# Two compression products of one transformer block: interleaved on two column halves of TensorE, or one after the other into one half

## The chip, the cores and the metric

One core of a Trainium2 chip runs the whole block. The metric is the device time of one execution in microseconds (us); lower is better. The engines are PE (TensorE), DVE (VectorE), ACT (ScalarE), POOL (GpSimd) and SP (SyncE, which issues most DMAs here). SBUF and PSUM have 128 partitions.

## The reference, cut to what matters

The block is a feed-forward layer, a token mixer and a second feed-forward layer over 512 tokens of width 1024, all in float32. In the mixer, keys and values of two KV groups are compressed: blocks of 32 tokens, 16 apart, become one key or value each (31 blocks per group), through a small two-layer network.

```
def compress(k, pos, w1, w2):
    b_, g_, s_, d_ = k.shape
    kc = k.reshape(b_, g_, s_ // CMP_STRIDE, CMP_STRIDE, d_)
    blocks = jnp.concatenate([kc[:, :, :-1], kc[:, :, 1:]], axis=3) + pos
    blocks = blocks.reshape(b_, g_, -1, CMP_BLOCK * d_)
    return jax.nn.gelu(blocks @ w1) @ w2
...
    kc = compress(k_cmp, cmp_pos_k, cmp_k_w1, cmp_k_w2)
    vc = compress(v_cmp, cmp_pos_v, cmp_v_w1, cmp_v_w2)
```

`blocks @ w1` has a contraction of 2048 (32 tokens times 64) and 256 hidden columns. The results feed a softmax attention over the 31 compressed blocks, one of three attention branches.

## The kernel before, in words

Activations lie feature by token: `h` is eight tiles of 128 features x 512 tokens. Weights stream in panels of 128 x 1024 float32 from HBM. ACT copies each panel into `w_hi` in a reduced format (fp32r) and POOL makes the remainder `w_lo` (L430); a product of full precision is three fp32r matmuls, `w_hi*h_hi`, `w_hi*h_lo`, `w_lo*h_hi` (L506 to L508). A panel over `h` is 24 such matmuls of 512 columns. Panels have four slots; SP loads, ACT and POOL split up to three panels ahead of PE.

The order of work is written out by hand per engine, with semaphores between them. In the mixer PE runs the panels `kc`, `vc`, `u0` to `u3`, then the compression's first layer (L696), the panel `gate`, the transposes of the hidden layer (L703), the panel `q0`, the second layer (L710, L714), the transposes of the gates (L721), `q1` to `q3`, the scores against the compressed keys (L731), more panels, and then the attention proper, in which PE, DVE, ACT and POOL hand tiles to each other (L761 scores, L812 transposes, L839 weighted sums).

The first layer works as follows. DVE writes `blocks` (L1487), in which partition is (parity of the token, feature) and the free dimension is (k or v and half of the block, pair of tokens, group and block). For each of the 16 pairs of tokens PE takes 64 columns of `blocks` as the stationary operand (31 blocks of each group and two columns that mean nothing) and streams `w1k` or `w1v`, 256 columns. The key product goes to partitions 0 to 63 of PSUM bank 2, the value product to partitions 64 to 127 of the same columns, and the code alternates key and value for every pair. These are float32 matmuls, not fp32r; each shows in the trace as two instructions.

The hidden layer is thus 128 x 256: rows are k then v. The tanh form of GELU follows on it: Square on ACT (L1099), two DVE operations (L1522, L1523), a Tanh on ACT with its table load (L1101), one DVE operation (L1526). PE waits for that (`cmp_act`) only after the panel `gate`. Two transposes of 128 x 128 (L703) put it into bank 3, and DVE copies it to `hidden` (L1528), which PE waits for after the panel `q0`.

Of the kernel before, what the change touches and what calls it, by code (L numbers as in the profile page):

```python
# [31 lines left out]
ALU = mybir.AluOpType  # L32
# [3 lines left out]
P = 128  # L36
# [8 lines left out]
HPG = HEADS // GROUPS  # L45
STRIDE = 16
N_CMP = T // STRIDE - 1
CPAD = 32
HID_T = 2
PAIRS = 16  # L50
# [74 lines left out]
def build(nc, xT, cols, ada_w, ada1, ffn_in, ffn_out, mix_w, pool_w, branch_w, mixout_w,  # L125
          w1, w2, pos, ident_in, dist_in, cbias_in, cmask_in, icnt_in, out):
    with ExitStack() as ctx:
        def at(name, shape, offset, dt=F32):
            return nc.alloc_sbuf_tensor_at(name, shape, dt, offset=offset)
# [11 lines left out]
        scr = at("scr", [P, 4, T], O_SCR)  # L141
# [7 lines left out]
        R = O_REGION  # L149
# [7 lines left out]
        V = at("V", [P, 2, TT, P], R + 12288)  # L157
        vT = at("vT", [P, 2, T], R + 16384)
        w1v = at("w1v", [P, PAIRS, 256], R)
        blocks = at("blocks", [P, 4 * 512 + 1], R + 20480)  # L160
        PT = at("PT", [P, 2, 2, PT_LEN], O_ADARAW)
        Pr = at("Pr", [P, 2, 2, P_LEN], R + 20480)
        pads = at("pads", [P, 4, 528], R + 30720)
        hidden = at("hidden", [P, 4, 64], R + 39168)
        cbias = at("cbias", [P, TT, HEADS, N_CMP], R + 40960)
        PcT = at("PcT", [P, GROUPS, T], R + 40960)
        dist = at("dist", [P, T], R + 45056)
        abias = [at("abias0", [P, 2, T], R + 47104), at("abias1", [P, 2, T], R + 16384)]
        Pc = at("Pc", [P, TT, HEADS, CPAD], R + 51200)
        cmask = at("cmask", [P, TT, CPAD], R + 55296)  # L170
        G = at("G", [P, TT, 24], R + 55808)
# [8 lines left out]
        w1k = at("w1k", [P, PAIRS, 256], R + 73728)  # L180
# [5 lines left out]
        ident = at("ident", [P, P], o)  # L186
# [7 lines left out]
        w2s = at("w2s", [P, 2, HID_T, HEAD], o + 2816)  # L194
        icnt = at("icnt", [P, 4, 16], o + 3840)
        kcB = at("kcB", [P, 2 * N_CMP], o + 4096)
        st = at("st", [P, 8, TT], o + 4352)
# [3 lines left out]
        psum = ctx.enter_context(nc.psum_tensor("psum", [P, 8, T], F32))  # L201

        def bank(n, w=T):
            return psum[:, n, 0:w]

        def sem(name):
            return ctx.enter_context(nc.semaphore(name))
# [70 lines left out]
        cmp_act = sem("cmp_act")  # L278
# [223 lines left out]
        def _(pe):  # L502
            def product(o_, wslot, kk, xh, xl, first, last):

                ws = slice(kk * P, (kk + 1) * P)
                pe.matmul(o_, w_hi[:, wslot, ws], xh, start=first, stop=False)  # L506
                pe.matmul(o_, w_hi[:, wslot, ws], xl, start=False, stop=False)  # L507
                return pe.matmul(o_, w_lo[:, wslot, ws], xh, start=False, stop=last)  # L508
# [180 lines left out]

            pe.wait_ge(mixc_landed, 16 * 5)  # L690
            pe.wait_ge(kv_blocks, 8)
            for i in range(PAIRS):
                half = i // 8
                for kv in range(2):
                    first = 512 * (2 * kv + half) + 64 * (i % 8) + half
                    ins = pe.matmul(psum[64 * kv:64 * kv + 64, 2, 0:256], blocks[:, first:first + 64],  # L696
                                    (w1k, w1v)[kv][:, i, :], start=(i == 0), stop=(i == PAIRS - 1))
            ins.then_inc(cmp_hidden, 1)
            k8_panel("gate")

            pe.wait_ge(cmp_act, 1)
            for kt in range(HID_T):
                ins = pe.transpose(psum[:, 3, P * kt:P * kt + P], scr[:, 0, P * kt:P * kt + P], ident[:, :])  # L703
            ins.then_inc(cmp_turned, 1)
            k8_panel("q0")

# [1 line left out]
            for g in range(GROUPS):  # L708
                for kt in range(HID_T):
                    pe.matmul(psum[64 * g:64 * g + 64, 2, 0:N_CMP], w2s[:, 0, kt, :],  # L710
                              hidden[:, 2 * kt, 32 * g:32 * g + N_CMP], start=(kt == 0), stop=(kt == 1))
            for g in range(GROUPS):
                for kt in range(HID_T):
                    ins = pe.matmul(psum[0:31, 2, 64 + 64 * g:128 + 64 * g],  # L714
                                    hidden[:, 2 * kt + 1, 32 * g:32 * g + N_CMP], w2s[:, 1, kt, :],
                                    start=(kt == 0), stop=(kt == 1))
            ins.then_inc(cmp_kv, 1)

# [1 line left out]
            for t in range(TT):  # L720
                ins = pe.transpose(psum[:, 4, P * t:P * t + P], vT[:, 0, t * P:(t + 1) * P], ident[:, :])  # L721
# [6 lines left out]
            for t in range(TT):  # L728
                for j in range(HPG):
                    col = ((t % 2) * HPG + j) * 2 * N_CMP  # L730
                    ins = pe.matmul(psum[:, 6 + t // 2, col:col + 2 * N_CMP], qT[:, j, t * P:(t + 1) * P],  # L731
                                    kcB[:, :], start=True, stop=True)
# [37 lines left out]
            for v in range(2):  # L770
                pe.wait_ge(act_evac, MIX8.index("vslc") - 1 + v)
                for t in range(TT):
                    ins = pe.transpose(psum[:, 2 + v, P * t:P * t + P], vT[:, v, t * P:(t + 1) * P], ident[:, :])
                ins.then_inc(v_turned, 1)

            p = pidx["poolw"]
            pe.wait_ge(split_done, p + 1)
            pe.wait_ge(pool_split, 4)
            for g in range(4):
                ins = product(bank(4 + g), p % 4, g, pool_hi[:, g, :], pool_lo[:, g, :], True, True)  # L780
# [5 lines left out]
            for g in range(GROUPS):  # L786
                pe.wait_ge(poolout_split, g + 1)
                for t in range(TT):
                    ins = pe.transpose(psum[:, 4 + g, P * t:P * t + P],
                                       Pc[:, t, HPG * g:HPG * g + HPG, :].rearrange("p h n -> p (h n)"),  # L790
                                       ident[:, :])
# [68 lines left out]
            for m in range(KT):  # L860
                p = B_BRANCH + 3 * m
# [17 lines left out]
                for k in range(4):  # L879
                    ins = product(bank(b + 3), p % 4, 4 + k, o_hi[:, k, :], o_lo[:, k, :], k == 0, k == 3)  # L880
# [3 lines left out]
            for m in range(KT):  # L884
                p = B_MIXOUT + m
# [5 lines left out]
                for k in range(KT):  # L891
                    if m == 0:
                        pe.wait_ge(br_split, k + 1)
                    ins = product(bank(m % 2), p % 4, k, mixed_hi[:, k, :], mixed_lo[:, k, :],
                                  k == 0, k == KT - 1)
# [7 lines left out]
        def _(act):  # L903
# [190 lines left out]
            act.wait_ge(pool_delta, 5)  # L1094
            act.activation(pool_hi[:, 3, :], pads[:, 3, 16:528], ACT.Copy).then_inc(pool_hi_done, 1)
            act.wait_ge(cmp_hidden, 1)
            hb = psum[:, 2, 0:256]
            sq = scr[:, 1, 0:256]
            act.activation(sq, hb, ACT.Square).then_inc(cmp_sq, 1)  # L1099
            act.wait_ge(cmp_arg, 1)  # L1100
            act.activation(sq, sq, ACT.Tanh, scale=GELU_A).then_inc(cmp_tanh, 1)  # L1101
# [85 lines left out]
        def _(dve):  # L1187
# [279 lines left out]
            def taken(name):  # L1467
                return B_MIX + MIX.index(name) + 1

            dve.wait_ge(h_split, 16)  # L1470
            for i in range(4):
                ins = dve.memset(pads[:, i, 0:16], 0.0)
            ins.then_inc(pool_delta, 1)
            dve.memset(Pc[:, :, :, N_CMP:CPAD], 0.0)
            dve.memset(blocks[:, 4 * 512:], 0.0)
            for kv, name in enumerate(("kc", "vc")):

                dve.wait_ge(panels_used, taken(name))
                for half in range(2):
                    for r in range(2):  # L1480
                        for g in range(GROUPS):
                            src = psum[64 * g:64 * g + 64, kv, r:T:2].rearrange("p (n i) -> p i n", i=8)
                            dst = blocks[64 * r:64 * r + 64, 0:4 * 512].rearrange("p (n i c) -> p n i c", n=4, c=64)\
                                [:, 2 * kv + half, :, 32 * g:32 * g + 32]
                            pp = posv[64 * r:64 * r + 64, kv:kv + 1, 8 * half:8 * half + 8]\
                                .rearrange("p o i -> p i o").broadcast_to([64, 8, 32])
                            ins = dve.tensor_tensor(dst, src, pp, ALU.add)  # L1487
                            if r == 1:
                                ins.then_inc(kv_blocks, 1)
            for g, w in enumerate(WINDOWS):  # L1490
# [25 lines left out]
            dve.tensor_tensor(pool_lo[:, 3, :], pads[:, 3, 16:528],  # L1516
                              pool_hi[:, 3, :].bitcast(F32), ALU.subtract).then_inc(pool_split, 1)

            hb = psum[:, 2, 0:256]
            sq = scr[:, 1, 0:256]  # L1520
            dve.wait_ge(cmp_sq, 1)
            link(dve.tensor_scalar(sq, sq, GELU_B, 1.0, ALU.mult, ALU.add))  # L1522
            dve.tensor_tensor(sq, sq, hb, ALU.mult).then_inc(cmp_arg, 1)  # L1523
            dve.memset(kcB[:, :], 0.0)
            dve.wait_ge(cmp_tanh, 1)
            dve.scalar_tensor_tensor(scr[:, 0, 0:256], sq, 1.0, hb, ALU.add, ALU.mult).then_inc(cmp_act, 1)  # L1526
            dve.wait_ge(cmp_turned, 1)
            dve.tensor_copy(hidden[:, :, :].rearrange("p n c -> p (n c)"), psum[:, 3, 0:256])\  # L1528
               .then_inc(cmp_hidden_T, 1)
            dve.wait_ge(cmp_kv, 1)  # L1530
            for g in range(GROUPS):
                rows = slice(64 * g, 64 * g + 64)
                ins = dve.tensor_scalar(kcB[rows, N_CMP * g:N_CMP * g + N_CMP], psum[rows, 2, 0:N_CMP], 0.5, None, ALU.mult)
            ins.then_inc(cmp_kv_taken, 1)
            for r in range(4):
                ins = dve.tensor_scalar(VC[32 * r:32 * r + 31, :], psum[0:31, 2, 64:192], 0.5, None, ALU.mult)
# [20 lines left out]
            for t in range(TT):  # L1557
                ins = dve.tensor_tensor(Pc[:, t, :, 0:N_CMP], Pc[:, t, :, 0:N_CMP], over_blocks(cst[:, 0, :], t), ALU.subtract)
# [7 lines left out]
            for t in range(TT):  # L1566
                ins = dve.tensor_tensor(Pc[:, t, :, 0:N_CMP], Pc[:, t, :, 0:N_CMP], over_blocks(cst[:, 2, :], t), ALU.mult)
            link(ins)
            for t in range(TT):
                ins = dve.tensor_tensor(Pc[:, t, :, 0:N_CMP], Pc[:, t, :, 0:N_CMP],  # L1570
                                        cmask[:, t:t + 1, 0:N_CMP].broadcast_to([P, 8, N_CMP]), ALU.mult)
# [118 lines left out]
def _constants():  # L1690
# [10 lines left out]
    cb = cb.reshape(TT, P, HEADS, N_CMP).transpose(1, 0, 2, 3)  # L1701
    cm = np.zeros((T, CPAD), np.float32)
    cm[:, :N_CMP] = d >= 0
    cm = cm.reshape(TT, P, CPAD).transpose(1, 0, 2)
    ic = np.stack([1.0 / np.minimum(np.arange(16) + 1, w) for w in WINDOWS]).astype(np.float32)
# [73 lines left out]
```

## Time and profile before

| | us |
|---|---|
| three runs | 1179.96, 1178.36, 1177.53 (median 1178.36) |
| profiled execution, its own time | 1179.96 |
| its span, first to last instruction | 1178.1 |
| PE busy | 1117.6 (95%) |
| POOL busy | 539.3 (46%) |
| DVE busy | 512.9 (44%) |
| ACT busy | 400.1 (34%) |
| mean granted TensorE clock | 0.973 |

The span ends 1.9 us short of the execution's own time. Busy time of PE counts from the first to the last moment at which any of its pipelined matmuls is open, so it says that PE had work, not that the array was full. PEld is the load of the stationary operand. An instruction's duration includes its way through the pipeline; how fast instructions follow each other is read from their start times. Shapes in PE rows read as stationary operand (partitions*columns), then the streamed operand (partitions x columns).

### The profile page before, as it was taken

To read this page: it belongs to the slowest core of one execution; us is meant where nothing else is said; L and a number is where in the kernel's file an instruction comes from. 1 tells how busy PE (TensorE), PEld (TensorE's weight loads), DVE (VectorE), ACT (ScalarE), POOL (GpSimd) and SP (SyncE) were. 2 spreads that over 40 slices of the span, in tenths; PEclk is the share of its full clock that TensorE was granted. 3 is DMA by queue.
4 is the path that set the end of the run, shared out by engine and by line. 5 is a ranking of instruction groups with operands and counts; after the bars stand their busy time and mean duration, and the time that the engine had idled before them with its cause. 6 is when DMAs were issued, how large, how long until landed. Compare 5 with 4: busy or idle time off the path is not lost.

```text
span 1178.1 us, 14475 instructions
## 1 busy us (share of the span) xinstructions
PE 1117.6 (95%) x5182; PEld 886.6 (75%) x5182; DVE 512.9 (44%) x830; ACT 400.1 (34%) x608; POOL 539.3 (46%) x268
## 2 busy tenths in 40 slices
PE   6999999999999889999999999969999999999992
PEld 3788888888888657875478888848888888888881
DVE  3567656321221366267837776661622222111116
ACT  3453323232222163247722333344423222222212
POOL 1334544444444363367725543544544544444423
PEclk8899999999999989999999999989999999999996
DMA  9446555323333522210036554313333333333311
GB/s 373 143 138 201 186 183 174 112 92 95 86 97 96 194 106 86 63 45 28 19 114 218 188 178 143 125 36 125 125 125 125 107 110 103 87 97 98 98 32 72
DMA packets 46991, 142.06 MB, mean 121 GB/s; under 512 B 5472, under 2 KB 5984, under 8 KB 45664
## 3 DMA queue, kind: packets, MB, share of 16 engines
q1 hardware_dynamic: 45504, 136.07, 34.9%
q10 hardware_dynamic: 1440, 5.35, 1.2%
q8 instruction: 30, 0.49, 0.2%
q14 instruction: 17, 0.14, 0.0%
HBM read 139.31 MB, written 2.10 MB: 120 GB/s over the span
## 4 chain that ended last, share of the span: by engine, by line
PE 76%; issue 10%; POOL 6%; DVE 5%; ACT 2%; DMA 1%; SPq 0%; POOLq 0%; ACTq 0%; DVEq 0%
PE psum L506 24%; PE psum L507 23%; PE psum L508 23%; POOL w_lo L430 3%; POOL Pr L465 1%; DMA ada_first<-in_ada 1%; POOL h_lo L488 1%; PE psum L590 1%; PE psum L537 1%; ACT Pr L1119 1%; PE psum L812 1%; PE psum L696 1%; DVE X L1290 1%; PE psum L523 0%; PE psum L761 0%
## 5 line engine op out<-in xcount | busy, mean ns | idle before, releaser
L430 POOL TENSOR_TENSOR w_lo<-raw,w_hi 128x1024 fp32r<-128x1024 f32 x184 | 452.4, 2462 | 551.9 <-ACT w_hi L916 551.5
L506 PE MATMUL psum<-h_hi,w_hi 128*128 128x512 f32 x952 | 375.8, 395 | 9.0 <-POOL h_lo L488 8.8
L507 PE MATMUL psum<-h_lo,w_hi 128*128 128x512 f32 x952 | 373.1, 392 | 0.0
L508 PE MATMUL psum<-h_hi,w_lo 128*128 128x512 f32 x952 | 372.9, 392 | 0.0
L916 ACT ACTIVATE w_hi<-raw 128x1024 fp32r<-128x1024 f32 x184 | 192.7, 1051 | 160.1 <-PE psum L508 104.0
L506 PEld LDWEIGHTS psum<-h_hi,w_hi 128*128 128x128 f32 x952 | 180.2, 189 | 55.3 <-POOL h_lo L488 9.2
L508 PEld LDWEIGHTS psum<-h_hi,w_lo 128*128 128x128 f32 x952 | 180.3, 189 | 38.0
L507 PEld LDWEIGHTS psum<-h_lo,w_hi 128*128 128x128 f32 x952 | 180.5, 190 | 36.4
L1318 DVE SCALAR_TENSOR_TENSOR acc<-ada_raw,cact,acc 128x512 f32<-128x512 f32 x98 | 138.3, 1447 | 19.0 <-DMA ada_raw<-in_ada_w 18.6
L506 PE MATMUL psum<-act_hi,w_hi 128*128 128x512 f32 x352 | 137.3, 390 | 0.0
L508 PE MATMUL psum<-act_hi,w_lo 128*128 128x512 f32 x352 | 137.0, 389 | 0.0
L507 PE MATMUL psum<-act_lo,w_hi 128*128 128x512 f32 x352 | 137.0, 389 | 0.0
L1386 DVE SCALAR_TENSOR_TENSOR X<-psum,mod,X 128x512 f32<-128x512 f32 x24 | 18.0, 750 | 217.3 <-PE psum L508 217.2
L1018 ACT ACTIVATE act_hi<-scr 128x512 f32 (+1 forms) x42 | 26.6, 632 | 187.3 <-DVE scr L1348 187.3
L1339 DVE SCALAR_TENSOR_TENSOR scr<-scr,psum 128x512 f32<-128x512 f32 x44 | 30.2, 686 | 123.6 <-ACT scr L1025 123.6
L508 PEld LDWEIGHTS psum<-act_hi,w_lo 128*128 128x128 f32 x352 | 66.1, 188 | 13.7
L507 PEld LDWEIGHTS psum<-act_lo,w_hi 128*128 128x128 f32 x352 | 66.1, 188 | 13.7
L506 PEld LDWEIGHTS psum<-act_hi,w_hi 128*128 128x128 f32 x352 | 66.1, 188 | 13.5
L1348 DVE TENSOR_TENSOR scr<-scr,psum 128x512 f32<-128x512 f32 x44 | 30.2, 686 | 89.0 <-PE psum L508 88.8
L1025 ACT ACTIVATE scr<-psum 128x512 f32<-128x512 f32 x44 | 26.1, 593 | 97.6 <-PE psum L508 97.6
L465 POOL TENSOR_SCALAR Pr<-Pr,pscl 128x128 f32<-128x128 f32 (+2 forms) x48 | 44.8, 950 | 19.2 <-DVE pscl L1594 19.2
L936 ACT ACTIVATE scr<-X 128x512 f32<-128x512 f32 x24 | 15.2, 634 | 104.8 <-DVE X L1386 104.8
(206 smaller groups left out, 986.0 us busy)
## 6 DMA issues: line engine op xcount, KB each, us to landing
raw<-in_ffn_in SPq DMA_DIRECT2D x88, 512.0 KB, 3.3
ada_raw<-in_ada_w SPq DMA_DIRECT2D x112, 256.0 KB, 3.6
raw<-in_mix_w SPq DMA_DIRECT2D x31, 512.0 KB, 3.3
raw<-in_ffn_out SPq DMA_DIRECT2D x32, 448.0 KB, 3.3
ada_first<-in_ada SPq DMA_DIRECT2D x8, 1024.0 KB, 16.2
raw<-in_ffn_out SPq DMA_DIRECT2D x16, 512.0 KB, 3.5
raw<-in_branch_w SPq DMA_DIRECT2D x8, 512.0 KB, 4.0
raw<-in_mixout_w SPq DMA_DIRECT2D x8, 512.0 KB, 3.3
```

The costliest lines, as they stand in the source:

```text
L430: gp.tensor_tensor(w_lo[:, slot, :], raw[:, slot % 2, :], w_hi[:, slot, :].bitcast(F32), ALU.subtract).then_inc(split_done, 1)
L465: gp.tensor_scalar(pr, pr, pscl[:, n:n + 1], None, ALU.mult).then_inc(probs_pool, 1)
L506: pe.matmul(o_, w_hi[:, wslot, ws], xh, start=first, stop=False)
L507: pe.matmul(o_, w_hi[:, wslot, ws], xl, start=False, stop=False)
L508: return pe.matmul(o_, w_lo[:, wslot, ws], xh, start=False, stop=last)
L916: act.activation(w_hi[:, slot, :], raw[:, slot % 2, :], ACT.Copy).then_inc(split_hi, 1)
L1018: act.activation(act_hi[:, c - 1, :] if isinstance(c, int) else act_hi[:, bass.ds(c - 1, 1), :].rearrange("p o t -> p (o t)"), scr[:, 1 - ...
L1025: act.activation(scr[:, c2, :], bank(2 * c2 if b is None else b), ACT.Tanh, scale=0.5).then_inc(tanh_done, 1)
L1318: dve.scalar_tensor_tensor(a, ada_raw[:, q % 3, :], sc, a, ALU.mult, ALU.add).then_inc(ada_used, 1)
L1339: dve.scalar_tensor_tensor(scr[:, c2, :], scr[:, c2, :], 1.0, bank(b0), ALU.add, ALU.mult).then_inc(gated, 1)
L1348: dve.tensor_tensor(scr[:, c2, :], scr[:, c2, :], bank(b0 + 1), ALU.mult).then_inc(hidden_made, 1)
L1386: dve.scalar_tensor_tensor(X[:, m, :], bank(y_bank + m % 2), mod[:, 4, m:m + 1], X[:, m, :], ALU.mult, ALU.add).then_inc(z_done, 1)
```

## The change

The two products are no longer interleaved. All 16 key matmuls run first, into partitions 0 to 62 and columns 0 to 255 of bank 2; then all 16 value matmuls into the same partitions and columns 256 to 511. The stationary operand has 63 columns (`CROWS`), not 64, so the memset of one spare element of `blocks` goes. The hidden layer is 63 x 512 and no longer 128 x 256, and the five GELU operations run on that shape. Its transposes are four of 63 x 128 rather than two of 128 x 128, and `hidden` is indexed as k0, k1, v0, v1. One line is added at the top of the file, so most later lines are one or two numbers further down.

```diff
+CROWS = 32 + N_CMP
...
-        blocks = at("blocks", [P, 4 * 512 + 1], R + 20480)
+        blocks = at("blocks", [P, 4, PAIRS // 2, 64], R + 20480)
...
-            for i in range(PAIRS):
-                half = i // 8
-                for kv in range(2):
-                    first = 512 * (2 * kv + half) + 64 * (i % 8) + half
-                    ins = pe.matmul(psum[64 * kv:64 * kv + 64, 2, 0:256], blocks[:, first:first + 64],
-                                    (w1k, w1v)[kv][:, i, :], start=(i == 0), stop=(i == PAIRS - 1))
+            for kv in range(2):
+                for i in range(PAIRS):
+                    half = i // 8
+                    ins = pe.matmul(psum[0:CROWS, 2, 256 * kv:256 * kv + 256],
+                                    blocks[:, 2 * kv + half, i % 8, half:half + CROWS], (w1k, w1v)[kv][:, i, :],
+                                    start=(i == 0), stop=(i == PAIRS - 1))
...
-            for kt in range(HID_T):
-                ins = pe.transpose(psum[:, 3, P * kt:P * kt + P], scr[:, 0, P * kt:P * kt + P], ident[:, :])
+            for n in range(4):
+                ins = pe.transpose(psum[:, 3, 64 * n:64 * n + CROWS], scr[0:CROWS, 0, P * n:P * n + P],
+                                   ident[0:CROWS, 0:CROWS])
...
-                              hidden[:, 2 * kt, 32 * g:32 * g + N_CMP], start=(kt == 0), stop=(kt == 1))
+                              hidden[:, kt, 32 * g:32 * g + N_CMP], start=(kt == 0), stop=(kt == 1))
...
-                                    hidden[:, 2 * kt + 1, 32 * g:32 * g + N_CMP], w2s[:, 1, kt, :],
+                                    hidden[:, 2 + kt, 32 * g:32 * g + N_CMP], w2s[:, 1, kt, :],
...
-            hb = psum[:, 2, 0:256]
-            sq = scr[:, 1, 0:256]
+            hb = psum[0:CROWS, 2, :]
+            sq = scr[0:CROWS, 1, :]
...
-            dve.memset(blocks[:, 4 * 512:], 0.0)
...
-            dve.scalar_tensor_tensor(scr[:, 0, 0:256], sq, 1.0, hb, ALU.add, ALU.mult).then_inc(cmp_act, 1)
+            dve.scalar_tensor_tensor(scr[0:CROWS, 0, :], sq, 1.0, hb, ALU.add, ALU.mult).then_inc(cmp_act, 1)
             dve.wait_ge(cmp_turned, 1)
-            dve.tensor_copy(hidden[:, :, :].rearrange("p n c -> p (n c)"), psum[:, 3, 0:256])\
+            dve.tensor_copy(hidden[:, :, 0:CROWS], psum[:, 3, 0:256].rearrange("p (n c) -> p n c", c=64)[:, :, 0:CROWS])\
```

On PE, at the first layer of the compression, the program had this before: the last matmul of panel `u3`, then the products with `w1k` and `w1v` in turn (32 in all; the first four and the last two stand here), then the panel `gate`.

```order
L508 MATMUL psum<-h_hi_50,w_lo_54 128x512
L696 MATMUL psum<-w1k_100,blocks_79 64x256
L696 MATMUL psum<-w1v_78,blocks_79 64x256
L696 MATMUL psum<-w1k_100,blocks_79 64x256
L696 MATMUL psum<-w1v_78,blocks_79 64x256
...
L696 MATMUL psum<-w1k_100,blocks_79 64x256
L696 MATMUL psum<-w1v_78,blocks_79 64x256
L506 MATMUL psum<-h_hi_50,w_hi_53 128x512
```

The same place of PE's program after the change, from the end of `u3` to the first product of `gate`:

```order
L508 MATMUL psum<-h_lo_51,w_hi_53 128x512
L509 MATMUL psum<-h_hi_50,w_lo_54 128x512
L696 MATMUL psum<-w1k_100,blocks_79 63x256 x16
L696 MATMUL psum<-w1v_78,blocks_79 63x256 x16
L507 MATMUL psum<-h_hi_50,w_hi_53 128x512
```

Sixteen pairs became two runs of sixteen; the count of matmuls and what lies around them is the same.

One panel later on PE, where the hidden layer (`scr`) is turned against the identity (`ident`), the program had before, between `gate` and `q0`:

```order
L506 MATMUL psum<-h_hi_50,w_hi_53 128x512
L507 MATMUL psum<-h_lo_51,w_hi_53 128x512
L508 MATMUL psum<-h_hi_50,w_lo_54 128x512
L703 MATMUL psum<-ident_104,scr_57 128x128 x2
L506 MATMUL psum<-h_hi_50,w_hi_53 128x512
```

and it has after the change:

```order
L507 MATMUL psum<-h_hi_50,w_hi_53 128x512
L508 MATMUL psum<-h_lo_51,w_hi_53 128x512
L509 MATMUL psum<-h_hi_50,w_lo_54 128x512
L704 MATMUL psum<-ident_104,scr_57 128x63 x4
L507 MATMUL psum<-h_hi_50,w_hi_53 128x512
```

Two transposes became four of 63 streamed columns each, at the same place.

## Rows read from the trace of the kernel before

**Rows 1.** The page: busy time by engine (us, share), and the last chain by engine.
```profile
PE 1117.6 (95%) x5182; PEld 886.6 (75%) x5182; DVE 512.9 (44%) x830; ACT 400.1 (34%) x608; POOL 539.3 (46%) x268
PE 76%; issue 10%; POOL 6%; DVE 5%; ACT 2%; DMA 1%; SPq 0%; POOLq 0%; ACTq 0%; DVEq 0%
```

**Rows 2.** PE in order of time: start us, duration us, line, tiles, shapes, count.
```profile
454.24 0.39 PE L508 MATMUL psum<-h_hi,w_lo 128*128 128x512 f32 x1
454.56 0.43 PE L696 MATMUL psum<-w1k,blocks 128*64 128x256 f32 x1
454.57 0.43 PE L696 MATMUL psum<-w1v,blocks 128*64 128x256 f32 x1
454.83 0.38 PE L696 MATMUL psum<-w1k,blocks 128*64 128x256 f32 x1
...
461.31 0.38 PE L696 MATMUL psum<-w1v,blocks 128*64 128x256 f32 x1
461.62 0.50 PE L506 MATMUL psum<-h_hi,w_hi 128*128 128x512 f32 x1
```

**Rows 3.** Groups of PE by shape: count, busy us, mean ns of one.
```profile
L696 PE MATMUL psum<-w1k,blocks 128*64 128x256 f32 x32 | 7.1, 381 | 0.0
L696 PE MATMUL psum<-w1v,blocks 128*64 128x256 f32 x32 | 7.1, 381 | 0.0
...
L839 PE MATMUL psum<-PT,V 128*64 128x384 f32 x32 | 6.5, 486 | 0.0
...
L839 PE MATMUL psum<-PT,V 128*64 128x128 f32 x32 | 3.1, 273 | 0.0
```

**Rows 4.** PE in order of time, around the two transposes.
```profile
466.28 0.39 PE L508 MATMUL psum<-h_hi,w_lo 128*128 128x512 f32 x1
...
466.96 0.39 PE L508 MATMUL psum<-h_hi,w_lo 128*128 128x512 f32 x1
467.20 0.38 PE L703 MATMUL psum<-ident,scr 128*128 128x128 f32 x2
...
467.64 0.39 PE L507 MATMUL psum<-h_lo,w_hi 128*128 128x512 f32 x1
```

**Rows 5.** PE in order of time, compressed scores with 62 streamed columns.
```profile
491.69 3.75 PE L731 MATMUL psum<-kcB,qT 128*128 128x62 f32 x32 [0.78 <-ACT qT L1108]
495.25 0.47 PE L506 MATMUL psum<-h_hi,w_hi 128*128 128x512 f32 x1
```

**Rows 6.** ACT in order of time, around the GELU.
```profile
454.67 0.60 ACT L1089 ACTIVATE pads<-psum 128x512 f32<-128x512 f32 x1 [3.37 <-PE psum L508]
...
461.74 0.38 ACT L1099 ACTIVATE scr<-psum 128x256 f32<-128x256 f32 x1 [1.04 <-PE psum L696]
462.14 1.28 ACT L1101 ACT_TABLE_LOAD   x1
463.43 0.42 ACT L1101 ACTIVATE scr<-scr 128x256 f32<-128x256 f32 x1
```

**Rows 7.** DVE in order of time, around the GELU.
```profile
459.13 0.69 DVE L1508 SCALAR_TENSOR_TENSOR pads<-scr,pads 128x512 f32<-128x512 f32 x1
...
462.48 0.42 DVE L1523 TENSOR_TENSOR scr<-scr,psum 128x256 f32<-128x256 f32 x1
...
463.88 0.42 DVE L1526 SCALAR_TENSOR_TENSOR scr<-scr,psum 128x256 f32<-128x256 f32 x1 [0.91 <-ACT scr L1101]
```

**Rows 8.** Stretch after the first layer: length, busy of PE, PEld, DVE, ACT, POOL; clock; DMA.
```profile
461.70:600.00 138.30, 130.31 (x740) 89.17 (x741) 79.21 (x243) 71.44 (x184) 82.67 (x67) 1.00 0.13 43
```

**Rows 9.** Longest wait of PEld in that stretch that another engine ends: total us, times, longest.
```profile
PEld psum L812 <- POOL Pr L465: 10.7, 19, 1.0
```

**Rows 10.** Stretches of PE alone: length, PE busy, granted clock, DMA share, GB/s.
```profile
457.00:460.00 3.00, 3.00 (x30) 1.00 0.03 11
...
410.00:415.00 5.00, 3.08 (x4) 0.50 0.99 426
...
420.00:425.00 5.00, 4.64 (x14) 0.78 0.00 0
```

More of the change, by code:

```diff
@@ L1482, in _ @@
                             src = psum[64 * g:64 * g + 64, kv, r:T:2].rearrange("p (n i) -> p i n", i=8)
-                            dst = blocks[64 * r:64 * r + 64, 0:4 * 512].rearrange("p (n i c) -> p n i c", n=4, c=64)\
-                                [:, 2 * kv + half, :, 32 * g:32 * g + 32]
+                            dst = blocks[64 * r:64 * r + 64, 2 * kv + half, :, 32 * g:32 * g + 32]
                             pp = posv[64 * r:64 * r + 64, kv:kv + 1, 8 * half:8 * half + 8]\
@@ L1517, in _ @@
                               pool_hi[:, 3, :].bitcast(F32), ALU.subtract).then_inc(pool_split, 1)
-            hb = psum[:, 2, 0:256]
-            sq = scr[:, 1, 0:256]
+            hb = psum[0:CROWS, 2, :]
+            sq = scr[0:CROWS, 1, :]
             dve.wait_ge(cmp_sq, 1)
```

## The prediction

> **What bounds the kernel now.** I read the page first. PE is busy for 95% of the span and carries 76% of the chain that ended last, the next engine 6% [rows 1]. So time added to PE's own program counts in full unless PE stood idle behind it for someone who would now be ready. Then PE in order of time around L696 [rows 2]. The panel `u3` ends with a matmul started at 454.24, the first key product and the first value product start at 454.56 and 454.57, the second key product at 454.83, the last value product at 461.31, and the panel `gate` at 461.62. PE does not wait inside this stretch. The reader is to see that a key and a value instruction start together.
>
> **Is this really two at once?** It decides everything, so it needs a second view. There are 32 instructions on `w1k` and 32 on `w1v` [rows 3], twice the 16 + 16 matmuls of the program. From the second key instruction (454.83) to the last value one (461.31) lie 30 steps of pairs: 6.48 / 30 = 0.216 us a step (starts are rounded, and the last pair starts with the last value row). Either one instruction takes 0.108 and the two go one after the other, or each takes 0.216 and they run side by side. The groups by shape decide. On the same kind of tile, L839 takes 273 ns with 128 streamed columns and 486 ns with 384; the 256 further columns cost 213 ns, and L696 with 256 columns stands at 381, on the same line [rows 3]. So streaming 256 float32 columns occupies a tile for 0.213 us, and 64 instructions fit into 7.06 us (461.62 - 454.56) only because two column halves stream at once. A slope of duration cannot be a delay that instructions share, so I trust it.
>
> By the Trainium skill's page "TensorEngine Tiling (Array Packing)", section "Key Properties", different tiles load and multiply in parallel; the trace agrees with its 0.01 us between the paired starts.
>
> **The change part by part.**
>
> 1. Products in one half. All 32 matmuls (64 instructions) now write from partition 0, so they share the same columns of the array and queue behind each other. Before, 32 steps of 0.215 (6.86 to 6.9 us); after, 64 steps. Added: 32 x 0.2145 = 6.9 us. Bounds of the step: 0.213, the pure streaming time, gives 6.8 with nothing lost; the upper end takes the spacing of the full panels, whose three matmuls from 466.28 to 466.96 take 0.227 each [rows 4]. They stream at a rate of their own, so only the excess over 0.213, 0.014 us, is carried over: 64 x 0.014 = 0.9 more, 7.8 in all. I take 6.9, since each column half already held 0.215 in the row that is the very operation. One column less in the stationary operand changes nothing, because it streams against the same 256 columns. The gaps at either end (454.24 to 454.56, 461.31 to 461.62) stay.
>
> 2. Transposes, four for two. From the last L508 of `gate` (466.96) to the second matmul of `q0` (467.64) are 0.68 us, where two ordinary steps take 0.45; so two transposes cost 0.23 [rows 4]. For instructions with few streamed columns and 128 stationary ones, L731 has a spacing of (495.25 - 491.69) / 32 = 0.111 us [rows 5]. Two more transposes at 0.111 add 0.22. They have 63 rows now, and PE's tiling may change around them; the trace's nearest row is the step from `u3` to L696, 0.32 instead of 0.227, which is 0.09 for a change of tiles [rows 2]. Two of those would bring 0.4. Lower end 0 (four times half the streamed columns), upper 0.5; I take 0.25.
>
> 3. GELU on 63 x 512. Time goes by elements per partition, which double. On ACT, 256 columns take 0.38 and 512 take 0.60 [rows 6]; on DVE 0.42 against 0.69 [rows 7]. The chain from the end of L696: Square 0.60, then the table load 1.28 side by side with two DVE operations, which at 0.6 + 0.69 now just fill it, Tanh about 0.62, the last DVE operation 0.69, and some 0.1 between them: 3.3 us, where it took 461.74 to 464.30, 2.6 us [rows 6, 7]. PE asks for it after `gate`, at 467.2, 5.5 us after the products [rows 4]. So 2.2 us of cover are left, and the cost is 0. Without that panel the 0.7 us would show. ACT's next weight copy stands behind the Tanh and moves some 0.4 us later; it is for a panel three ahead of PE. Cost 0.
>
> 4. The copy to `hidden`, 252 elements for 256, covered by the panel `q0`; the memset of one element that goes, DVE long before. 0.
>
> 5. What is given back. From 461.7 to 600 PE is busy 130.3 of 138.3 us [rows 8], so 8 us of idleness could in principle take up the 6.9. But I read its largest case, PE's transposes L812 waiting for POOL's scaling L465, 19 times and at most 1.0 us each [rows 9]; that scaling waits for scores that PE itself makes two steps earlier. All of it moves with PE. Weight panels are split three ahead of PE and PE did not wait for one here. Given back: 0, at most 0.5.
>
> Sum: 6.9 + 0.25 = 7.15 us. The profiled execution would go from 1179.96 to 1187.1, its span from 1178.1 to 1185.25. That execution was the highest of three, 1.6 above the median; the forecast is for a median, 1178.36 + 7.15 = 1185.5.
>
> **Rivals.**
>
> A. The pairs were never side by side: one instruction occupies PE for 0.108 us, and order alone changes. Then L696 stays at 7 us and only the transposes add 0.25, with 1178.6 as the time. Against it stands the slope of 213 ns per 256 columns [rows 3]. 3%.
>
> B. Serial loads. In one column half a stationary operand may have to wait for the matmul in flight. L731 is bound by such loads: 0.111 us for 128 columns, so 0.056 for 63 [rows 5]. Then a step is 0.214 + 0.056 = 0.27, 64 steps 17.3 us, and the change 17.3 - 6.9 + 0.25 = +10.7, at 1189.0. Against it: the panels' 128-column loads would make their step 0.213 + 0.111 = 0.32, and it is 0.227 [rows 4]; and L696 shows 0.215 within each half. 5%. The Trainium skill, "TensorE: Matmul & The Clock Gate", section "The mechanism", states this rule: loads overlap a matmul in flight only where the row group differs, and here all rows are the same ones. The panels of this trace speak against it.
>
> C. The clock. With one half of the columns at work the granted clock may fall to its lower level, 1.2 GHz. From 410 to 415 us the granted clock was 0.50, which is that level, while PE was busy 3.08 of 5 us; in L696, without a gap, it was 1.00 [rows 10]. What lowers it here goes with pauses, and the change brings none; no row shows half the columns at work for 14 us. If it fell in the middle, the second half of the products takes 6.9 us more; when PE resumed after its pause around 410 us, the stretch from 420 to 425 had 0.78 [rows 10], so over 1 us is lost at the return, say 2. Total +7.15 + 9 = 16 us, at 1194.5. 5%.
>
> D. Given back, so not slower. PE's 8 idle microseconds after 461.7 [rows 8] would be waits for work that does not depend on PE's position, with POOL behind on splitting weights and late with its scaling. Then PE arriving 6.9 later finds all ready. To end below the time before, it would have to return over 7.15 of the 8.0, and it decides from the point at which POOL is idle before L465; POOL is busy 82.7 of 138.3 us there [rows 8], so it is not behind. It would give 1178.36 + 7.15 - 8.0 = 1177.5. 1%. A part of this, some 3 us given back (1182.5), 3%.
>
> **How the numbers follow.** The forecast (rigid shift, 6.8 to 8.3 us) has 83%, A 3, B 5, C 5, D 4. Terms at their ends: 6.8 + 0 - 0.5 = 6.3 and 7.8 + 0.5 = 8.3, which is 1184.7 to 1186.7. Three runs before spread by 2.4 us, so a median is uncertain by about 1 on both sides of the comparison: 1183.6 to 1188.1. A range from 1183.5 to 1188.3 leaves out most of B, all of A, C and D. No change that a measurement can tell is within 0.2%, 2.4 us. Slower by more: forecast, B, C and the mild part of D, 95%; within: A and noise, 4%; faster 1%.
>
> **What the profile after would show.** L696 as two blocks of 32 instructions each, with no two starts together, spacing 0.213 to 0.227, and 13.7 to 14.6 us from its first start to the first of `gate`. Spacing 0.27 is B, a granted clock under 1.00 there is C, 7 us in all is A. Step 2: from the last matmul of `gate` to the second of `q0` 0.9 us rather than 0.68. Step 3: the last GELU operation ends about 3.3 us after L696, and PE has no wait before the transposes; a wait there would make it wrong. Step 5: from the transposes to the end of the span all distances as before, and PE idle again about 8 us in the same stretch. The forecast is wrong if the span grows by less than 6 or more than 9 us.

## The result

The changed kernel takes 1185.21 us (median of four runs, 1184.42 to 1186.39), the kernel before, run beside it, 1177.94 us (median of four, 1177.31 to 1179.96): +7.27 us, a ratio of 1.0058 with a 95% interval of 1.0044 to 1.0073, which is 5.2 to 8.6 us. The forecast was +7.15, at 1185.5. The profiled execution took 1185.08 us, with a span of 1183.2.

### The profile page after: what moved, and what is told of

Same layout as the page of the kernel before. It is cut to its first block, busy times and chain, and to the rows that moved or that the text cites. A ratio compares the mean times of both kernels' runs of the same rounds, so it can differ in the third digit from the quotient of the medians.

```text
span 1183.2 us, 14478 instructions
## 1 busy us (share of the span) xinstructions
PE 1121.2 (95%) x5184; PEld 887.8 (75%) x5184; DVE 513.9 (43%) x829; ACT 400.5 (34%) x608; POOL 539.6 (46%) x268
## 4 chain that ended last, share of the span: by engine, by line
PE 87%; DVE 5%; ACT 2%; POOL 2%; issue 2%; DMA 2%; SPq 0%; ACTq 0%; DVEq 0%; POOLq 0%
PE psum L507 27%; PE psum L508 27%; PE psum L509 27%; DMA raw<-in_ffn_in 2%; PE psum L696 1%; POOL Pr L466 1%; POOL h_lo L489 1%; PE psum L591 1%; ACT Pr L1121 1%; PE psum L814 1%; PE psum L841 1%; PE psum L538 1%; DVE X L1292 1%; PE psum L524 1%; PE psum L763 0%
## 5 line engine op out<-in xcount | busy, mean ns | idle before, releaser
L508 PEld LDWEIGHTS psum<-act_lo,w_hi 128*128 128x128 f32 x352 | 66.1, 188 | 13.6
L1332 DVE TENSOR_TENSOR act_lo<-scr,act_hi 128x512 f32 (+1 forms) x44 | 37.1, 843 | 36.2 <-ACT act_hi L1020 34.8
```

Source lines behind the costliest of these rows:

```text
L1332: dve.tensor_tensor(lo_, scr[:, b, :], hi.bitcast(F32), ALU.subtract).then_inc(act_split, 1)
```

## The profile after, beside the rows of before

PE in order of time, at the first layer of the compression (start us, duration us, line, tiles, shapes, count; equal neighbours are merged into one row):

```profile
452.93 7.12 PE L696 MATMUL psum<-w1k,blocks 128*63 128x256 f32 x32
459.89 7.07 PE L696 MATMUL psum<-w1v,blocks 128*63 128x256 f32 x32
466.89 0.50 PE L507 MATMUL psum<-h_hi,w_hi 128*128 128x512 f32 x1
```

It answers to [rows 2]. The two kinds no longer start together: 32 key instructions, then 32 value instructions. From the first of them to the first matmul of `gate` are 13.96 us, where it was 7.06. One step is 13.96 / 64 = 0.218 us with the gap at the end counted in, and (459.89 - 452.93) / 32 = 0.2175 without it; each column half had 0.216 before.

PE, ACT and DVE after that, up to the transposes:

```profile
472.23 0.39 PE L509 MATMUL psum<-h_hi,w_lo 128*128 128x512 f32 x1
472.55 0.46 PE L704 MATMUL psum<-ident,scr 63*128 63x63 f32 x4
472.94 0.50 PE L507 MATMUL psum<-h_hi,w_hi 128*128 128x512 f32 x1
473.27 0.39 PE L508 MATMUL psum<-h_lo,w_hi 128*128 128x512 f32 x1
```

```profile
467.00 0.59 ACT L1101 ACTIVATE scr<-psum 63x512 f32<-63x512 f32 x1 [7.93 <-PE psum L696]
467.60 1.28 ACT L1103 ACT_TABLE_LOAD   x1
468.90 0.63 ACT L1103 ACTIVATE scr<-scr 63x512 f32<-63x512 f32 x1
```

```profile
467.62 0.42 DVE L1522 TENSOR_SCALAR scr<-scr 63x512 f32<-63x512 f32 x1 [7.83 <-ACT scr L1101]
468.07 0.68 DVE L1523 TENSOR_TENSOR scr<-scr,psum 63x512 f32<-63x512 f32 x1
469.56 0.68 DVE L1526 SCALAR_TENSOR_TENSOR scr<-scr,psum 63x512 f32<-63x512 f32 x1 [0.74 <-ACT scr L1103]
```

From the last matmul of `gate` to the second of `q0` are now 1.04 us (472.23 to 473.27); in [rows 4] they were 0.68. The GELU runs from 467.00 to 470.24, 3.24 us; in [rows 6, 7] it took 2.56. It ends 2.3 us before PE asks for it, so PE waits for nothing.

The stretch of 138.3 us that follows `gate`'s start, in the form of [rows 8]:

```profile
466.90:605.20 138.30, 130.33 (x741) 89.03 (x741) 79.83 (x243) 71.70 (x183) 82.67 (x67) 1.00 0.14 43
```

PE is busy 130.33 us of it, before 130.31, and its wait for POOL's scaling, the one of [rows 9], is 10.2 us in 18 pieces. Nothing was given back in this stretch.

For comparisons finer than a run's spread I use one distance within a trace: from the first product of the first layer to the first score against the compressed keys. Before, 454.56 [rows 2] to 491.69 [rows 5] is 37.13 us; after, 452.93 to 497.32 is 44.39. The difference is 7.26 us. That the medians differ by 7.27 is agreement within their interval of 5.2 to 8.6; the match of the last digit is luck. The spans differ by only 5.1 us, for two other reasons. The profiled execution after reached the first layer 1.63 us earlier, in a part where the two programs are alike and where the granted clock fell and came back at other moments (18 to 21 us: 1.00 where it was 0.50 before the change; 29 to 59 us: 0.91 against 0.88). And from the scores to the end it took 0.5 us less: one wait of PE for a weight panel split by POOL, 0.3 us, is missing, as it also is in e11 below, and the rest arises around 790 us, where the clock falls while PE pauses. All distances below are from the first product to the first score.

## The experiments

The theory was the forecast's: two products run together because of their place, that is, because they lie in different column halves of the array. Rivals were order (alternation as such), serial loads of the stationary operand, and the clock.

**Both in one half, but alternating (e3).** The changed kernel with the loops exchanged and the value product in bank 3 (the GELU then reads both banks; those lines are left out here):

```diff
-            for kv in range(2):
-                for i in range(PAIRS):
+            for i in range(PAIRS):
+                for kv in range(2):
...
-                    ins = pe.matmul(psum[0:CROWS, 2, 256 * kv:256 * kv + 256],
+                    ins = pe.matmul(psum[0:CROWS, 2 + kv, 0:256],
```

> The changed kernel, with key and value products alternating as before the change, but both in the same column half; the value product goes to PSUM bank 3 instead of the upper half of bank 2. Theory (place): as slow as the changed kernel, first layer 13.9 us, 7.2 us slower than before. Rival (order): what the change lost is the alternation, for instance because two products on one accumulator in a row wait for each other; then the first layer is near 7.1 us here and the kernel near the time of before.

Measured: ratio to before 1.0077 (1.0060 to 1.0094), distance 44.39, as in the changed kernel, first layer 13.96 us. PE in order of time:

```profile
451.06 0.65 PE L696 MATMUL psum<-w1k,blocks 128*63 128x256 f32 x2
451.54 0.59 PE L696 MATMUL psum<-w1v,blocks 128*63 128x256 f32 x2
451.97 0.59 PE L696 MATMUL psum<-w1k,blocks 128*63 128x256 f32 x2
452.40 0.59 PE L696 MATMUL psum<-w1v,blocks 128*63 128x256 f32 x2
```

The reader sees that a float32 product is two instructions, and that each pair of one kind starts 0.43 us (the first time 0.48) after the pair of the other kind, never with it. Alternation alone brings nothing; place is needed.

**Both halves kept, order changed (e1, e2, e10, e11).** The kernel before, with turns of 16, 4, 8 and 2 products:

```diff
-            for i in range(PAIRS):
-                half = i // 8
+            for c in range(0, PAIRS, 16):
                 for kv in range(2):
...
+                    for i in range(c, c + 16):
+                        half = i // 8
```

This is e1; e2, e10 and e11 have 4, 8 and 2 in place of 16.

> The kernel before, both column halves of the array kept, but all 16 key products first and then all 16 value products. Theory (place): what makes two products run together is that they lie in different column halves. How far apart they may stand in PE's program is open. If PE starts instructions strictly in order, no value product starts before the last key product has started; the first layer then takes 63 steps of 0.215 = 13.6 us instead of 7.06, and the kernel is 6.6 us slower than before. If PE can reach over 32 queued instructions, the first layer stays at 7.1 us and the kernel at the time of before. Rival (order is nothing, place is all) predicts 7.1 us.

> The kernel before, both column halves kept, in turns of 4 key products and 4 value products. Strictly in order with one instruction open per half: each turn of 8 instructions per half overlaps with the other half only at its edges, where the last key and first value instruction start together; 64 starts less 7 shared ones = 57 steps of 0.215, 12.2 us, the kernel about 5.2 us slower than before. If PE reaches over 8 instructions but not over 32, it is 7.1 us here and 13.6 us with turns of 16.

> The kernel before, both column halves kept, in turns of 8 key and 8 value products. Theory drawn from the turns of 16 and 4: PE starts an instruction of the other half over 3 queued ones of its own, so at each of the 3 borders between turns 4 instructions of each half run side by side; 64 - 3 x 4 = 52 steps, 11.2 us of first layer and 4.1 us more than before. Rival (a reach that ends between 8 and 32 instructions): all turns up to some length near 7.1 us.

> The kernel before, both column halves kept, in turns of 2 key and 2 value products, which is 4 instructions each. Theory (reach over 3 queued instructions): every step has a partner but for the first and last few; 32 steps and 1 to 4 more, first layer 7.1 to 7.9 us, kernel within 0.9 us of before. Rival (strictly in order): 64 - 15 = 49 steps, 10.5 us.

| products per turn | first layer us | distance us | to before | ratio (95%) |
|---|---|---|---|---|
| 1 (before) | 7.06 | 37.13 | | |
| 2 (e11) | 7.11 | 37.19 | +0.06 | 0.9992 (0.9979 to 1.0004) |
| 4 (e2) | 8.31 | 38.41 | +1.28 | 1.0010 (1.0000 to 1.0020) |
| 8 (e10) | 11.54 | 41.62 | +4.49 | 1.0033 (1.0012 to 1.0053) |
| 16 (e1) | 13.15 | 43.23 | +6.10 | 1.0067 (1.0050 to 1.0083) |

So place is needed but does not suffice: with both halves in use, turns of 16 lose nearly all that the change loses. By the device times e1 is even further from before (ratio 1.0067, about 7.9 us); its profiled execution shows why that can be: behind the scores, outside the distance, the granted clock fell to 0.50 for some 6 us (498 to 505) and 2.8 us were lost, which no other profiled execution of this table shows. PE around the border between the two turns of e1:

```profile
452.94 6.47 PE L697 MATMUL psum<-w1k,blocks 128*64 128x256 f32 x29
459.04 0.43 PE L697 MATMUL psum<-w1v,blocks 128*64 128x256 f32 x1
459.25 0.38 PE L697 MATMUL psum<-w1k,blocks 128*64 128x256 f32 x1
459.31 0.38 PE L697 MATMUL psum<-w1v,blocks 128*64 128x256 f32 x1
459.46 0.38 PE L697 MATMUL psum<-w1k,blocks 128*64 128x256 f32 x1
459.52 0.38 PE L697 MATMUL psum<-w1v,blocks 128*64 128x256 f32 x1
459.68 0.38 PE L697 MATMUL psum<-w1k,blocks 128*64 128x256 f32 x1
459.74 6.42 PE L697 MATMUL psum<-w1v,blocks 128*64 128x256 f32 x29
```

and at the start of e2:

```profile
453.92 1.29 PE L697 MATMUL psum<-w1k,blocks 128*64 128x256 f32 x5
454.84 0.43 PE L697 MATMUL psum<-w1v,blocks 128*64 128x256 f32 x1
455.05 0.38 PE L697 MATMUL psum<-w1k,blocks 128*64 128x256 f32 x1
```

In e1 the first value instruction starts with key instruction 29 of 32 and ahead of three that precede it in the program; in e2 with number 5 of 8, again ahead of three. For e1 a strict order had given 13.6 us, the measured first layer is 13.15. For e2 both values of the expectation were wrong, 12.2 us by a strict order and 7.1 if PE reaches over 8; the measured 8.31 lies between. The rule "ahead of at most three queued instructions of the other half" was drawn from these two and then forecast turns of 8: 52 steps, 11.2 us. e10 gave 11.54, and its first value instruction starts with key instruction 13 of 16:

```profile
454.97 3.02 PE L697 MATMUL psum<-w1k,blocks 128*64 128x256 f32 x13
457.62 0.43 PE L697 MATMUL psum<-w1v,blocks 128*64 128x256 f32 x1
```

e11 lay inside its 7.1 to 7.9. The count of steps leaves out two things. Before the change 32 steps of 0.215 are 6.9 us and the first layer takes 7.06, so about 0.2 belongs to its two ends. And every border between turns costs about 0.06 us more: in e1 the value stream follows 0.06 us behind the key stream. With both, e10 comes to 11.2 + 0.2 + 3 x 0.06, e2 (36 steps, 7 borders) to 8.3 and e1 (60 steps, one border) to 13.1, all within 0.1 us of what was measured.

**One kind of product nearly left out (e4, e5).** Of the 16 value products only the first is done, in the kernel before (e4, first pair of lines) and in the changed one (e5, second pair); the compressed values are then not the reference's.

```diff
-                for kv in range(2):
+                for kv in range(2 if i == 0 else 1):
...
-                for i in range(PAIRS):
+                for i in range(PAIRS if kv == 0 else 1):
```

> The kernel before without 15 of the 16 value products (the compressed values are then not the reference's). Theory: they ran beside the key products, so leaving them out saves nothing: first layer 6.9 to 7.1 us, kernel within 0.3 us of before. Rival (the pair was one after the other at 0.108 each): the first layer falls to 3.6 us and the kernel is 3.3 us faster.

> The changed kernel without 15 of its 16 value products (the compressed values are then not the reference's). Theory: each was a step of its own, 30 instructions of 0.215, so it is 6.5 us faster than the changed kernel and 0.8 us slower than before (the two steps left of the value, and four transposes for two). Rival (they are hidden in part): less than 6 us is saved.

In the kernel before, the distance is 37.12, 0.01 less than with all products (ratio 1.0003, 0.9993 to 1.0013): 15 products left out, nothing saved. In the changed kernel it falls from 44.39 to 37.91, by 6.48 us for 30 instructions, 0.216 each. That is 0.8 us more than the distance before, as expected; the device times (ratio 0.9998, 0.9986 to 1.0010) can't tell it from before. PE in e4 and in e5:

```profile
452.01 0.43 PE L696 MATMUL psum<-w1k,blocks 128*64 128x256 f32 x1
452.01 0.43 PE L696 MATMUL psum<-w1v,blocks 128*64 128x256 f32 x1
...
452.49 6.64 PE L696 MATMUL psum<-w1k,blocks 128*64 128x256 f32 x30
459.06 0.50 PE L506 MATMUL psum<-h_hi,w_hi 128*128 128x512 f32 x1
```

```profile
461.07 0.59 PE L696 MATMUL psum<-w1v,blocks 128*63 128x256 f32 x2
461.60 0.50 PE L507 MATMUL psum<-h_hi,w_hi 128*128 128x512 f32 x1
```

Rival A, that the pairs were never side by side, is ruled out by e4: at 0.108 us each the 30 instructions left out would have saved 3.2 us.

**Products doubled (e6).** The changed kernel with each run of 16 done twice, `for kv in (0, 0, 1, 1):`.

> The changed kernel with each run of 16 products done twice (the second overwrites the first). Theory: 64 more instructions of 0.213 to 0.217, 13.7 us more than the changed kernel, about 20.9 us more than before, with the granted clock at 1.00 throughout the 27.6 us. Rival (clock): with half the columns at work for so long the granted clock falls to the lower level somewhere in the stretch; the added time is then over 16 us, up to 27, and steps of 0.43 us appear.

Ratio 1.0171 (1.0154 to 1.0188), distance 58.20: 13.81 us more than the changed kernel for 64 instructions, 0.216 each. The granted clock in the stretch (length, PE busy, clock, DMA share, GB/s):

```profile
455.00:460.00 5.00, 5.00 (x25) 1.00 0.09 33
...
475.00:480.00 5.00, 5.00 (x25) 1.00 0.00 0
```

With half the columns at work for 27.8 us, twice as long as in the changed kernel, the clock stays at its upper level, 2.4 GHz. Rival C has no ground, and at 0.216 a step rival B (0.27) has none either.

**Transposes repeated (e9; one run).** `for n in (0, 1, 2, 3) * 3:` in the changed kernel.

> The changed kernel with its four transposes done three times in a row (twelve, on the same places). The changed kernel's distance from the last matmul of gate to the second of q0 is 1.04 us, before it was 0.68. If a transpose costs 0.06 to 0.07 (load of 128 columns from 63 rows being short) and the rest is the change of tiles at both ends, eight more add 0.5; if each costs 0.11, as the spacing of L731 has it, they add 0.9 and the distance is 1.9 us.

```profile
471.06 0.39 PE L509 MATMUL psum<-h_hi,w_lo 128*128 128x512 f32 x1
471.38 0.96 PE L704 MATMUL psum<-ident,scr 63*128 63x63 f32 x12
472.27 0.50 PE L507 MATMUL psum<-h_hi,w_hi 128*128 128x512 f32 x1
472.60 0.39 PE L508 MATMUL psum<-h_lo,w_hi 128*128 128x512 f32 x1
```

The distance from `gate` to the second matmul of `q0` grows from 1.04 to 1.54: 0.06 us for each transpose of 63 streamed columns. Four cost 0.25. Of the 1.04, two ordinary steps take 0.45 and the transposes 0.25. The 0.34 that is left does not grow with their number; it lies at the two ends. The step into them is 0.32 us, as into L696 [rows 2], where the step into the two 128*128 transposes before was 0.24 [rows 4]. That the 0.34 comes from the change of tiles is the likely reading; no run changes the tiles alone.

**Without the cover of the GELU (e7, e8; one run each).** In each kernel `k8_panel("gate")` is moved behind the transposes.

> The kernel before with the panel gate moved behind the two transposes, so that nothing covers the GELU. PE then waits for it: from the last product to the first transpose about 2.6 us (the chain 461.74 to 464.30) + 0.3, and of the 5.5 us of cover nothing is used: kernel 2.7 to 3.2 us slower than before.

> The changed kernel with the panel gate moved behind the four transposes. PE's wait for the GELU shows its length on 63 x 512: 3.3 us + 0.3, so 0.7 us more wait than the same move gives in the kernel before, and 10.5 us more than the kernel before in all. If the chain on 63 partitions were as short as on 128 x 256, the wait is 2.6 + 0.3.

The waits of PE in e7 and in e8 (waiter, whom for, total us, times, longest):

```profile
PE psum L702 <- DVE scr L1526: 2.7, 1, 2.7
```

```profile
PE psum L703 <- DVE scr L1526: 3.3, 1, 3.3
```

The wait is 0.66 us longer on 63 x 512 (3.33 against 2.67), as step 3 had it. e7's distance is 39.81, +2.68, just its wait. e8's is 49.21, +4.82 over the changed kernel and +12.08 to before, where +10.5 was expected; 1.5 of it is not the wait. The stretches of PE in e8 (start and end, length, PE busy, clock, DMA share, GB/s) show why:

```profile
467.60:471.30 3.70, 0.42 (x2) 1.00 0.00 0
471.30:472.50 1.20, 1.15 (x7) 1.00 0.00 0
472.50:474.00 1.50, 1.50 (x5) 0.52 0.00 0
474.00:475.50 1.50, 1.50 (x5) 0.50 0.26 76
475.50:477.00 1.50, 1.50 (x7) 0.85 0.70 273
477.00:480.00 3.00, 3.00 (x15) 1.00 0.00 0
```

After PE had stood still and about 1 us into its next work, the granted clock fell to its lower level, 1.2 GHz, and stayed there for about 3 us, which costs the 1.5 us. In e7 PE stood 0.66 us less and the granted clock stayed at 1.00 up to the scores. But it fell there, for some 6 us, where before the change it was 1.00:

```profile
498.00:500.00 2.00, 2.00 (x7) 0.50 0.00 0
504.00:506.00 2.00, 2.00 (x11) 1.00 0.00 0
```

That lies outside the distance and costs 2.7 us, so e7's device time was missed: 1184.06 us, 5.3 over the median of before, where 2.7 to 3.2 was expected. The pause of PE just before the scores is 0.78 us in e7, in e1, which fell at the same place, and in the kernel before [rows 5], which did not. These are single executions, and neither the length of a pause nor the program tells by itself when such a fall comes.

## Why the prediction was right

1. Step 1, products in one half: 6.9 forecast, 6.90 measured (13.96 - 7.06). The mechanism was right as far as it went. e4 and e5 show the mechanism directly, since a value product cost nothing before and 0.216 us per instruction after. What I had not asked was whether place is the whole of it. It isn't: e1 keeps both halves and still loses 6.10 us, and a forecast by place alone would have been wrong for it by all of that. The change took away both conditions at once, place and nearness in the program; losing place alone costs as much as the change (e3), losing nearness alone most of it (e1).
2. Step 2, transposes: 0.25 forecast, 0.36 measured, within the 0 to 0.5. The price of one was too high (0.111 from L731, which streams 62 columns but loads 128 rows of 128 columns; measured 0.06), so four of them cost 0.25, hardly more than the 0.23 of two before. Of the 0.25 taken, 0.22 was for the two more transposes, which left 0.03 for the two ends, where 0.34 was measured; the text had named up to 0.18 for them. The two errors were of opposite sign, and that the step came out near its forecast is luck. The Trainium skill, "TensorEngine Tiling (Array Packing)", section "Key Properties", says that a change of tiling mode drains the engine. The 0.08 us more on the way in (0.32 against 0.24) are in line with it; no row shows the drain itself.
3. Step 3, GELU: chain 3.3 us forecast, 3.24 measured, with 2.3 us of cover left (forecast 2.2). Its cost was 0, and e7 and e8 put 0.66 on it without the cover (forecast 0.7).
4. Step 4, the copy and the memset: PE waits for neither; 0.
5. Step 5, given back: 0. PE's idle time in the stretch after is the same to 0.02 us, so rival D fails. The reason given, that those waits move with PE, fits the wait for POOL's scaling (10.7 us before, 10.2 after); no run tests it by itself. The 0.5 us less behind the scores is not shown to come from the change: e11, as fast as the kernel before, has 0.3 of it too.

The sum, 7.15, lies 0.1 from what was measured, both as a distance and as a difference of medians. The distances bear that out; the medians are uncertain by more than 1 us, so their part of the agreement is luck.

Of the rivals, A falls by e4, B and C by e6. Beside B stood a rule of the Trainium skill ("TensorE: Matmul & The Clock Gate", section "The mechanism"), that a load overlaps a matmul in flight only where row groups differ; the same section also lets a load go ahead where it targets the background weight buffer. In this kernel all rows are the same ones and the step was 0.216 us, not 0.27, so the load of 63 columns was hidden, against the rule as it was applied.

## What to carry to other kernels

Two narrow products of this kind (float32, all 128 rows, 63 or 64 columns) ran side by side on TensorE only where they lay in different column halves and also stood close together in its program; here turns of up to four instructions cost next to nothing (0.06 us), and turns of 32 gave away nearly the whole gain. A group of rows that start together, and a slope of duration over streamed columns, tell from one trace whether products run side by side; leaving one kind out then proves it. Where PE has no wait, its added instructions count in full, and a distance between two fixed instructions of one trace measures them more finely than the span, but it does not see what follows behind its end, such as the fall of the clock in e1 and e7. No kernel here beats the one before beyond what its interval can tell; turns of two came out equal to it.

## What was not expected of the hardware

PE started a matmul ahead of three earlier ones in the program, when those queued for the other column half: with key instruction 29 of 32 (e1) and 5 of 8 (e2). That reach of three held in turns of 2, 4, 8 and 16 products, and at every border between turns in e2 and e10. Whether it counts instructions, or loads and matmuls together, or depends on the shape, was not tried. A transpose of 63 x 128 into 128 x 63 costs 0.06 us in a row of them. And the 3.33 us of waiting in e8 were followed by some 3 us at the lower clock, the 2.67 us in e7 were not, while in e1 and e7 a pause of 0.78 us before the scores was followed by some 6 us at the lower clock, which the same pause in the kernel before was not.
